# Block attention's probabilities multiplied by their reciprocal sums on GpSimd in a one-layer hybrid decoder kernel

## What is computed

```
x = x + 0.5 * swiglu_ffn(x, ...)                         # FFN 1, hidden width 2816
h = rms_norm(x); P = h @ w_in
y_gdn  = gated_deltanet(...)                             # 4 heads x 128, chunked delta rule
y_moba = moba_attention(...)                             # 4 heads x 64, causal, blocks of 256, ALiBi
y_mem  = memory_attention(...)                           # 4 heads x 64 into 256 memory tokens
x = x + concat(y_gdn, y_moba, y_mem) @ w_out
x = x + 0.5 * swiglu_ffn(x, ...)                         # FFN 2
```

```
s = q @ k^T * scale - slope * distance
p = softmax(s);  out = p @ v
```

## Time and profile before

| what | value |
|---|---|
| median of 3 runs | 1003.11 us (1002.99 to 1003.37) |
| the profiled execution's own time | 1002.87 us |
| its span in the trace | 1001.1 us |
| TensorE clock granted | 1.0 of full speed throughout |
| stage from 557 to 606 us | block attention, levels of pair 1 and scan |

### The profile page before, as it was taken

How to read it: one execution, slowest core, us unless ns; L and a number is a source line. 1 busy time by engine, 2 the same in 40 slices (tenths; PEclk the granted TensorE clock), 3 DMA queues, 4 the chain that set the end, 5 groups by cost and what they waited for, 6 DMA issues and landing times.

```text
span 1001.1 us, 16467 instructions
## 1 busy us (share of the span) xinstructions
PE 994.9 (99%) x6826; PEld 876.2 (88%) x6826; DVE 688.7 (69%) x1084; ACT 440.0 (44%) x645; POOL 505.1 (50%) x289
## 2 busy tenths in 40 slices
PE   9999999999999999999999999999999999999998
PEld 7888999999999988788878788888899999999997
DVE  5896986766666486863547883687688776667745
ACT  7542543344433462444356664534244244443341
POOL 0364866667566433543252201635576675756741
PEclk9999999999999999999999999999999999999999
DMA  8332223331233212321221001223302332123312
GB/s 331 127 127 84 85 84 127 127 126 51 82 121 127 99 71 85 122 89 43 85 69 61 2 3 43 95 89 112 126 32 96 127 127 104 65 85 127 127 43 84
DMA packets 15770, 95.32 MB, mean 95 GB/s; under 512 B 2000, under 2 KB 2128, under 8 KB 5456
## 3 DMA queue, kind: packets, MB, share of 16 engines
q1 hardware_dynamic: 15696, 94.27, 26.4%
HBM read 92.16 MB, written 2.10 MB: 94 GB/s over the span
## 4 chain that ended last, share of the span: by engine, by line
PE 92%; DVE 3%; DMA 1%; ACT 1%; POOL 1%; SPq 0%; issue 0%; DVEq 0%; POOLq 0%
PE bank L1916 50%; PE bank L2044 32%; DMA raw<-stream 1%; POOL wlo L485 1%; PE bank L2336 1%; PE bank L2340 1%; PE bank L2450 1%; PE bank L2384 1%; PE bank L2362 1%; PE bank L2422 0%; PE bank L2439 0%; ACT sqx L606 0%; PE bank L2406 0%; PE bank L2396 0%; ACT whi L581 0%
## 5 line engine op out<-in xcount | busy, mean ns | idle before, releaser
L485 POOL TENSOR_TENSOR wlo<-raw,whi 128x1024 fp32r<-128x1024 f32 (+1 forms) x44 | 148.3, 3387 | 215.2 <-ACT whi L581 198.4
L2044 PE MATMUL bank<-t_ffn_hi,wlo 128*128 128x256 f32 x896 | 253.6, 283 | 0.0
L2044 PE MATMUL bank<-t_ffn_lo,whi 128*128 128x256 f32 x896 | 253.6, 283 | 0.0
L2044 PE MATMUL bank<-t_ffn_hi,whi 128*128 128x256 f32 x896 | 253.5, 283 | 0.0
L502 POOL TENSOR_TENSOR wlo<-sums,whi 128x512 fp32r<-128x512 f32 x128 | 170.4, 1354 | 120.3 <-ACT whi L695 120.1
L502 POOL TENSOR_TENSOR wlo<-raw,whi 128x512 fp32r<-128x512 f32 x96 | 158.7, 1667 | 39.3 <-ACT whi L695 39.3
L2044 PEld LDWEIGHTS bank<-t_ffn_lo,whi 128*128 128x128 f32 x896 | 172.0, 192 | 0.6
L2044 PEld LDWEIGHTS bank<-t_ffn_hi,whi 128*128 128x128 f32 x896 | 172.0, 192 | 0.6
L1916 PE MATMUL bank<-ahi,whi 128*128 128x512 f32 x432 | 171.2, 396 | 1.0 <-POOL wlo L485 1.0
L2044 PEld LDWEIGHTS bank<-t_ffn_hi,wlo 128*128 128x128 f32 x896 | 172.0, 192 | 0.0
L1916 PE MATMUL bank<-ahi,wlo 128*128 128x512 f32 x432 | 168.4, 390 | 0.0
(11 more groups left out here) (312 smaller groups left out, 1408.2 us busy)
## 6 DMA issues: line engine op xcount, KB each, us to landing
raw<-fast_in SPq DMA_DIRECT2D x32, 1024.0 KB, 4.9
raw<-stream SPq DMA_DIRECT2D x30, 1024.0 KB, 4.9
raw_down<-fast_in SPq DMA_DIRECT2D x18, 1024.0 KB, 7.0
raw<-stream SPq DMA_DIRECT2D x6, 512.0 KB, 6.3
x<-x_in SPq DMA_DIRECT2D x4, 512.0 KB, 6.9
out<-x SPq DMA_DIRECT2D x8, 256.0 KB, 2.0
raw<-stream SPq DMA_DIRECT2D x4, 256.0 KB, 6.1
memx<-mem_in SPq DMA_DIRECT2D x2, 512.0 KB, 10.6
```

The lines of the kernel that those rows point to most:

```text
L485: ins = nc.gpsimd.tensor_tensor(wlo[:, u % RING, c0:c1], raw[:, u % RAW, c0:c1], whi[:, u % RING, c0:c1].bitcast(F32), ALU.subtract)
L2044: ins = E.matmul(psum[bank][:, HALF * h:HALF * (h + 1)], a, b[:, k, :], start=start and k == 0 and m == 0, stop=k == K2 - 1 and m == 2, sk ...
```

## The change

GpSimd takes over the multiplication of `prob`: VectorE's `scale(p, e)` keeps only the reciprocal and signals `inv_ready`; a new `scale(p, e)` on GpSimd waits for that and multiplies. Its sixteen calls are put between the masks of pair 1 in a fixed order. Apart from this, the semaphores `ab_sem` and `masks_in` become one, `tables_in`, for which both readers wait until both loads are there.

```
-            sp.dma_start(abr[:], ab_in).then_inc(ab_sem, 16)
-            sp.dma_start(cst[:, C_LEV:C_SEL], const_in[:, C_LEV:C_SEL]).then_inc(masks_in, 16)
+            sp.dma_start(abr[:], ab_in).then_inc(tables_in, 16)
+            sp.dma_start(cst[:, C_LEV:C_SEL], const_in[:, C_LEV:C_SEL]).then_inc(tables_in, 16)
...
-            pool.wait_ge(masks_in, 16)
+            pool.wait_ge(tables_in, 32)
...
-            for l in range(LAST):
-                masks(1, l)
+            def scale(p, e):
+                a = 2 * (NM + p) + e
+                m4 = slice(a % 4, a % 4 + 1)
+                tile = prob[a % 4][:, 0:P * (p // 2 + 1)]
+                pool.wait_ge(inv_ready, 2 * p + e + 1)
+                nc.gpsimd.tensor_scalar(tile, tile, rowinv[:, m4], None, ALU.mult).then_inc(pr_ready, 1)
+
+            masks(1, 0)
+            scale(0, 0)
+            scale(0, 1)
+            masks(1, 1)
+            scale(1, 0)
+            scale(1, 1)
+            masks(1, 2)
+            scale(2, 0)
+            scale(2, 1)
+            masks(1, 3)
+            scale(3, 0)
+            masks(1, 4)
+            scale(3, 1)
+            masks(1, 5)
+            for p in range(4, 8):
+                scale(p, 0)
+                scale(p, 1)
...
-            act.wait_ge(ab_sem, 16)
+            act.wait_ge(tables_in, 32)
...
             def scale(p, e):
                 a = 2 * (NM + p) + e
-                scaled(a, prob[a % 4][:, 0:P * (p // 2 + 1)])
+                m4 = slice(a % 4, a % 4 + 1)
+                dve.wait_ge(exp_done, a + 1)
+                V.reciprocal(rowinv[:, m4], rowsum[:, m4]).then_inc(inv_ready, 1)
```

More of the change, by code:

```diff
@@ L294, in gcol @@
             return gates[:, n, h * NC_ + c:h * NC_ + c + 1]
-        cst_in, masks_in, small_sem, ab_sem, out_done = (
-            sem(n) for n in ("cst_in", "masks_in", "small_sem", "ab_sem", "out_done"))
+        cst_in, tables_in, small_sem, out_done = (
+            sem(n) for n in ("cst_in", "tables_in", "small_sem", "out_done"))
+        inv_ready = sem("inv_ready")
         mem_sems = [sem(f"mem_in{i}") for i in range(2)]
```

## The result

The changed kernel takes 1004.77 us in the median (1004.17 to 1005.40, 20 runs) against 1003.00 us before (1002.50 to 1003.37, 20 runs): a ratio of 1.0017, 95% interval 1.0011 to 1.0024. It is 1.77 us slower. The forecast was 1003.3 us with a range to 1004.6 us; the median lies 0.17 us outside it.

What follows compares the result with a forecast made beforehand. TensorE, busy 994.9 of 1001.1 us, bounds the kernel. Terms -0.35 + 0.51 + 0 = +0.16 us on the profiled execution's 1002.87 us gave 1003.3 us predicted, range 1002.5 to 1004.6 us.

Steps and rivals of the forecast that it cites:

- The early gain: TensorE's order by 565.4 us: waits for VectorE's run up to level_update(1, 1) shrink, -0.35 us.
- The semaphore: ScalarE also waits for the larger load, there by about 26.1 us, reader at 29.80: costs nothing, 3.7 us of cover.
- Steps 5 and 6: Block attention's steps 5 and 6: scaling falls into gaps of GpSimd, hidden by TensorE's other groups.
- Step 7: Last tile (7, 1) before its second four transposes: free up to 1.69 us for one multiplication.
- rival 5: VectorE and GpSimd hinder each other on SBUF, one operation hit at most: +0.5 us, 1003.6 us; chance 0.05.
- rival 4: One-off cost of GpSimd's first call, paid beyond 1.87 us; about 6 us would add some 4 us; chance 0.03.
- The price of one multiplication: On GpSimd, half the two-input slope, same start: 0.32, 0.46, 0.59, 0.73 us for 128, 256, 384, 512 columns.
- signs of being wrong: 512 columns over 1.8 us, a group other than level_first(1, 3) waiting long for GpSimd, or level_first(1, 2) not earlier.
- rival 1: Two-input or dearest-split price, x for 256 and y for 384 columns: 1003.8 to 1004.6 us; chance 0.20.
- rival 3: GpSimd becomes the bound: price k times the two-input line, over 2 us slower at k = 1.4, 1005.2 us; chance 0.07.
- `level_first(1, 3)` against before: Mask of level 3 behind scale(2, 1) on GpSimd: 256-column price minus 0.30, +0.16 us net.
- step 4: Two 384-column multiplications on GpSimd before turn(4, 1): free up to 0.87 us each, so 0 at 0.59 us.

Runs made afterwards that it cites:

- e9: Kernel before with the multiplication by the reciprocal left out, output not normalized: 1002.85 us, ratio 0.9997.
- e1: Kernel before with only the shared semaphore for the two small loads: 1003.05 us, ratio 0.9998.
- e12: e8 with only the last tile, (7, 1), multiplied a second time by 1.0: 1004.52 us, ratio 1.0014.
- e4: Changed kernel with the two multiplications of step 4 back on VectorE: 1003.98 us, ratio 1.0009.
- e2: Changed kernel with the two separate semaphores back, multiplications still on GpSimd: 1004.59 us, ratio 1.0015.
- e8: Changed kernel with masks(1, 3) ahead of scale(2, 1) and VectorE's reciprocals of step 4 issued earlier: 1003.06 us, ratio 1.0001.
- e10: e8 with all sixteen multiplications written as tensor_tensor with a broadcast column: 1002.84 us, ratio 0.9998.
- e11: e8 with both tiles of step 7 multiplied a second time by 1.0: 1007.00 us, ratio 1.0037.

## Why the prediction was wrong

**What held.** TensorE's order set the end, and the changed kernel's loss was paid in the two places the prediction named, in GpSimd's order ahead of `masks(1, 3)` and at `turn(4, 1)`. The early gain was there: predicted 0.35 us by `level_first(1, 2)`, measured 0.23. The prediction had taken all but 0.17 of the 0.33 us of idle time before `level_first(1, 1)` for a wait; it stayed even in e9 (first row), and in the kernel before the same 0.33 us stand ahead of `turn(1, 0)`, which waited for nothing (second row). Both groups come directly behind a group of `scores` of 256 columns.

```profile
561.60 0.56 PEld L2338 LDWEIGHTS bank<-xn,bm 64*64 64x64 f32 x32 [0.33 <-DVE xn L1639]
```

```profile
564.84 0.20 PEld L2439 LDWEIGHTS bank<-cst,prob 128*128 128x128 f32 x2 [0.33 <-issue]
```

The semaphore cost nothing that e1 can see. Steps 5 and 6 cost nothing. Step 7 was hidden with a limit near the 1.69 us given, though only just: 1.56 us of work fitted, and e12 shows the limit by passing it. Two SBUF inputs on VectorE beside GpSimd (rival 5) did not show: the two operations of that kind, at 587.29 and 594.99 us, met GpSimd for 0.14 and 0.11 us only and took 0.68 us each. No one-off first-call cost (rival 4) showed: the first multiplication took 0.61 us like the others of its width, and started 0.14 us behind its mask.

**What failed.** The price of one multiplication, the step "the new operation reads one tensor in place of two, so I take half the slope and the same start". It gave 0.46, 0.59 and 0.73 us for 256, 384 and 512 columns; measured are 0.93, 1.24 and 1.56. With them the wait at `turn(4, 1)`, which the prediction had put at nothing, was there, and that was one of its own signs of being wrong. The rule of the Trainium skill that the prediction drew on beside it (GPSIMD Engine Reference, section 4.1, Engine selection) pointed the same way, and the measurement decides against both: 1.56 us for 512 columns on GpSimd, 0.49 on VectorE. The error went into the chances as well: the case that came is rival 1 at its dear end (x = 0.95 and y = 1.31, against 0.93 and 1.24), rival 1 as a whole had 0.20, and the range ended at that rival's 1004.6 us with nothing for other terms. A smaller slip: rival 3's own formula gives 1.9 us at k = 1.4, not over 2; nothing here hangs on it.

The prediction's own formulas with the measured prices give it back:

| term | by the formula, predicted price | by the formula, measured price | measured |
|---|---|---|---|
| `level_first(1, 3)` against before | +0.16 | 0.93 - 0.30 = +0.63 | 17.43 - 16.61 = +0.82 |
| step 4 | 0 | 2 x 1.24 - 1.75 = +0.73 | 48.69 - 47.93 = +0.76 (after against e4) |
| later gain of VectorE's freed time | 0 | 0 | (46.85 - 30.20) - (47.23 - 30.43) = -0.15 |
| sum | +0.16 | +1.36 | 48.69 - 47.23 = +1.46 |

The difference of 0.19 us in the first row is 0.12 us of early gain that did not come, 0.05 us because GpSimd started 0.25 us after the reciprocal's start and not 0.20, and 0.05 us because TensorE's weight load started 0.10 us after the mask's end and not 0.05, less 0.03 us because this multiplication and this mask took 0.92 and 1.25 us in place of 0.93 and 1.27. Of the 0.15 us in the third row, a term that the prediction put at nothing, the gain is between `turn(5, 0)` and `turn(6, 0)` (3.39 us in e9, 3.58 before). The three measured terms add to 1.43 us against 1.46, good to their reading.

**What stays open.** With the measured price the formula gives 1.36 us, that is 1004.5 us, which is still inside the stated range. The medians differ by 1.77 us in 20 runs each and by 1.52 us for e2; the stage explains 1.46. Part of the rest lies outside the span of the trace. Each run's own time is longer than its span, in the kernel before, e1 and e9 by 1.79 to 1.80 us in the mean, and in the kernels that multiply on GpSimd by 1.91 to 2.10 us (the changed kernel 1.95, e2 2.00, e8 2.01; these means are good to 0.02 us). So 0.1 to 0.3 us comes with the multiplications on GpSimd and not with the semaphore, and no view shows what it is. It closes e2: its spans are 1.32 us longer than those of the kernel before in the same set, and 0.20 us more lies outside. The last 0.1 to 0.2 us of the changed kernel's 1.77 is within what the starts ahead of the stage scatter.

**Why there was nothing to win.** The change took 5 us off VectorE, and 0.38 us of that mattered. Part of this small gain goes again outside the span. e8's spans are 0.20 us shorter than those of the kernel before in the same set, and its runs have 0.22 us more outside it, so its median is the old one. e10 is 0.34 us shorter by its spans and has 0.15 us more outside, and is within the measurement of the kernel before.

## What to carry to other kernels

Before moving an operation to another engine, find a row of that very form on that engine, or keep the dearest form in the range with something to spare: here one input was not cheaper than two. Moving work off an engine that isn't the bound can win only the idle time that the bound shows it owes to that engine; everything on the receiving engine's in-order queue behind the new waits can lose more. When it does, look at the order first: the same sixteen operations at the same price lengthened the stage by 1.5 us or shortened it by 0.26, depending on where one mask and two reciprocals stood.

## What the runs showed of the hardware

GpSimd's `tensor_scalar` on fp32 took 2.49 ns a column plus 0.29 us with a factor from SBUF, 2.49 plus 0.21 with a constant, and the same multiplication as `tensor_tensor` with a broadcast column 1.67 plus 0.19. VectorE did it in 0.29 to 0.49 us.

TensorE's granted clock stayed at 2.4 GHz behind idle times of its weight loads of 0.89, 1.10 and 1.64 us in this stage. Behind one of 2.43 us it was at 1.2 GHz for about 3 us in e11's profiled execution. Of e11's five executions four have a mean clock of 0.998, this one among them, and 1006.83 to 1007.96 us; the fifth had 1.000 and 1005.04 us. So a wait here can cost more than its length: 2 us lay between the two outcomes of one kernel.
